# Gate and up matmuls of a two-layer trunk: the high and low part of x side by side under one weight tile

## The chip, the cores and the metric

The kernel runs on one core of a Trainium2 chip. What counts is the device time of one execution in microseconds (us), from the start of the program to its end. Of the core's engines, TensorE (PE) does matmuls into PSUM, VectorE (DVE) and ScalarE (ACT) work element by element, GpSimd (POOL) does a few slow side jobs and issues some loads, and SyncE (SP) issues the weight loads. They run side by side and wait for each other by semaphores only.

## What is computed

A trunk of two layers on 256 tokens of 1,024 channels, all in float32. Each layer has a feed-forward block, a token mixer (pooling in the first layer, windowed attention in the second) and a second feed-forward block, each with a residual and a layer norm. Four feed-forward blocks with an inner width of 2,816 hold most of the work:

```python
def swiglu(x, w_gate, w_up, w_down):
    h = jax.nn.silu(x @ w_gate) * (x @ w_up)
    return h @ w_down

for i in range(DEPTH):
    x = post_norm(x, 0.5 * swiglu(x, ffn_w_gate[i, 0], ffn_w_up[i, 0], ffn_w_down[i, 0]), ln_g[i, 0], ln_b[i, 0])
    ...   # mixer and its norm
    x = post_norm(x, 0.5 * swiglu(x, ffn_w_gate[i, 1], ffn_w_up[i, 1], ffn_w_down[i, 1]), ln_g[i, 2], ln_b[i, 2])
```

## The kernel before

**Three matmuls for one.** A float32 product is made from reduced-precision pieces (type fp32r): ScalarE rounds a tile to its high part, VectorE subtracts to get the low part, and TensorE adds up high x high, high x low and low x high. The helper `three` (lines 1056 to 1059) does this: line 1057 is w_hi with x_hi, line 1058 w_hi with x_lo, line 1059 w_lo with x_hi. The stationary operand of gate and up is a 128x128 weight tile, the moving one x transposed, 256 tokens wide.

**Units.** The inner width is cut into 22 units of 128 channels. For unit u of a block f, `gate_up(f, u)` makes the gate (m = 0) and the up half (m = 1), each over 8 tiles of 128 channels k: 2 x 8 x 3 = 48 matmuls of 256 columns, both halves into one PSUM bank, `WORK + u % 2`. `ffn_down(f, u)` multiplies h by the down weights into the accumulator banks 0 to 3: 12 matmuls of 512 columns. Units 0 and 1 use the unsplit weights (`gate_up_raw`), whose outputs go to the same banks as the others'.

**Order on the engines.** It is written out by hand. TensorE runs gate_up(u) and then ffn_down(u-1), with a loop over units 2 to 17 and the last four written out; there the down parts are halved by token tile, so that after gate_up(20) only half a down part and gate_up(21) stand before the down part of unit 20. Beside it ScalarE makes, per unit, SiLU of the gate (line 471), the two high halves of unit u+2's gate and up weights (459), the high part of h (475) and of the next down weights (467). VectorE makes the product with up (728), the two low halves (720), the low part of h (733) and of the down weights (724). Semaphores tie them: `g_used` counts finished gate and up parts, `silu_done`, `hf_done`, `h_hi_done` and `h_lo_done` the steps of h; ffn_down waits for `h_lo_done`, and a gate_up waits for `hf_done` of the unit two before it, whose PSUM bank it takes. SyncE loads the next pair of units' weights when `g_lo_done` or `d_lo_done` says that a buffer is free.

**GpSimd** scales the pool weights (line 335) when they have landed, which is near the end of the first block, and then gb (341, 345); their load is issued once `d_lo_done` has reached the low part of unit 19's down weights.

**Between blocks** x is normalised, transposed by TensorE (`transposes`, line 1123, into banks 6 and 7) and split into xT_hi and xT_lo.

## Time and profile before

| | us |
|---|---|
| three runs | 917.87, 919.07, 919.52 |
| median | 919.07 |
| span of the profiled execution, first to last instruction | 916.1 |
| TensorE busy in it | 875.6 (96%) |
| VectorE busy | 540.4 (59%) |
| ScalarE busy | 380.1 (41%) |
| GpSimd busy | 76.3 (8%) |

The profiled execution is told by its span; its own time is not listed beside the three runs, whose median lies 3.0 us above the span. The mean granted clock of TensorE over the span is 0.992 of full speed (2.4 GHz). Records of matmuls overlap, and their ends are modelled, so the pace of TensorE is read from one start to the next, and not from the duration shown.

### The profile page before, as it was taken

How to read it: one execution, taken by the hardware profiler on the slowest of the kernel's cores; microseconds unless marked ns; L12 is line 12 of the kernel's file. 1: busy time of each engine (PE TensorE's matmuls, PEld its weight loads, DVE VectorE, ACT ScalarE, POOL GpSimd, SP SyncE). 2: the span in 40 equal slices, each digit the busy share in tenths (PEclk: the TensorE clock that was granted, in tenths of full speed). 3: DMA queues.
4: the chain of work that ended last, by engine and by line, in shares of the span. 5: the costliest groups of instructions: out<-in, count | busy, mean ns of one | idle time of the engine just before them, and what ended most of it. 6: DMA issues, size and time to landing. Idle time of an engine off the chain costs nothing.

```text
span 916.1 us, 14933 instructions
## 1 busy us (share of the span) xinstructions
PE 875.6 (96%) x5954; PEld 805.0 (88%) x5954; DVE 540.4 (59%) x758; ACT 380.1 (41%) x622; POOL 76.3 (8%) x71
## 2 busy tenths in 40 slices
PE   6999999997999999999999999988999999999995
PEld 6999999986999999998999999976766899999994
DVE  1764455488674455447665545568687775445445
ACT  2444344322444344333434433435575434434430
POOL 0020000066100000001040000023000100000001
PEclk9999999999999999999999999999999999999998
DMA  9886546254485555660865565450127096555501
GB/s 293 304 289 219 183 160 207 97 176 141 170 301 184 197 172 181 211 202 2 275 239 184 173 217 175 161 218 15 42 101 254 20 311 234 183 189 177 184 1 46
DMA packets 116275, 162.30 MB, mean 177 GB/s; under 512 B 3968, under 2 KB 97760, under 8 KB 116240
## 3 DMA queue, kind: packets, MB, share of 16 engines
q1 hardware_dynamic: 112656, 152.06, 49.2%
q0 software_dynamic: 2496, 9.44, 2.8%
q8 instruction: 24, 0.39, 0.2%
q10 hardware_dynamic: 1088, 0.32, 0.1%
q14 instruction: 11, 0.09, 0.0%
HBM read 160.75 MB, written 1.05 MB: 177 GB/s over the span
## 4 chain that ended last, share of the span: by engine, by line
PE 82%; DVE 10%; ACT 3%; POOL 2%; issue 1%; DMA 1%; SPq 0%; POOLq 0%; DVEq 0%; ACTq 0%
PE ps L1057 25%; PE ps L1058 25%; PE ps L1059 25%; PE ps L1073 5%; DVE stats L759 2%; DVE xn L758 2%; DMA raw_g<-in_ffn_w_up 1%; POOL rstd L356 1%; DVE xn L774 1%; PE ps L1123 1%; PE ps L943 1%; ACT silu L403 1%; PE ps L934 1%; PE ps L937 1%; POOL rstd L358 1%
## 5 line engine op out<-in xcount | busy, mean ns | idle before, releaser
L1059 PE MATMUL ps<-xT_hi,g_lo 128*128 128x256 f32 x1280 | 362.2, 283 | 0.0
L1058 PE MATMUL ps<-xT_lo,g_hi 128*128 128x256 f32 x1280 | 362.2, 283 | 0.0
L1057 PE MATMUL ps<-xT_hi,g_hi 128*128 128x256 f32 x1280 | 361.8, 283 | 0.0
L1057 PEld LDWEIGHTS ps<-xT_hi,g_hi 128*128 128x128 f32 x1280 | 245.4, 192 | 3.2
L1058 PEld LDWEIGHTS ps<-xT_lo,g_hi 128*128 128x128 f32 x1280 | 245.4, 192 | 3.1
L1059 PEld LDWEIGHTS ps<-xT_hi,g_lo 128*128 128x128 f32 x1280 | 245.4, 192 | 0.0
L720 DVE TENSOR_TENSOR g_lo<-raw_g,g_hi 128x1024 fp32r<-128x1024 f32 x171 | 206.5, 1247 | 42.0 <-ACT g_hi L459 41.9
L471 ACT ACTIVATE silu<-ps 128x256 f32<-128x256 f32 x88 | 33.8, 384 | 393.0 <-PE ps L1059 386.1
L728 DVE TENSOR_TENSOR hf<-silu,ps 128x256 f32<-128x256 f32 x88 | 37.0, 421 | 263.0 <-ACT silu L471 263.0
L459 ACT ACTIVATE g_hi<-raw_g 128x1024 fp32r<-128x1024 f32 x172 | 172.0, 1052 | 4.9 <-PE ps L943 4.4
L1057 PE MATMUL ps<-d_hi,hT_hi 128*128 128x512 f32 x352 | 138.7, 394 | 2.0 <-DVE hT_lo L733 2.0
L1058 PE MATMUL ps<-d_lo,hT_hi 128*128 128x512 f32 x352 | 137.9, 392 | 0.0
L1059 PE MATMUL ps<-d_hi,hT_lo 128*128 128x512 f32 x352 | 137.0, 389 | 0.0
L724 DVE TENSOR_TENSOR d_lo<-raw_d,d_hi 128x1024 fp32r<-128x1024 f32 x98 | 122.8, 1254 | 2.6 <-ACT d_hi L467 2.6
L467 ACT ACTIVATE d_hi<-raw_d 128x1024 fp32r<-128x1024 f32 x98 | 102.7, 1049 | 3.1 <-PE ps L1059 3.0
L1059 PEld LDWEIGHTS ps<-d_hi,hT_lo 128*128 128x128 f32 x352 | 66.1, 188 | 14.5
L1057 PEld LDWEIGHTS ps<-d_hi,hT_hi 128*128 128x128 f32 x352 | 66.4, 189 | 14.0 <-DVE hT_lo L733 2.4
L1058 PEld LDWEIGHTS ps<-d_lo,hT_hi 128*128 128x128 f32 x352 | 66.4, 189 | 10.6
L1073 PE MATMUL ps<-xf,raw_g 128*128 128x128 f32 x512 | 61.7, 282 | 3.8 <-DMA raw_g<-in_ffn_w_up 3.2
L1073 PEld LDWEIGHTS ps<-xf,raw_g 128*128 128x128 f32 x512 | 60.1, 197 | 5.4 <-DMA raw_g<-in_ffn_w_up 3.4
L733 DVE TENSOR_TENSOR hT_lo<-hf,hT_hi 128x256 fp32r<-128x256 f32 x88 | 43.5, 494 | 5.3 <-ACT hT_hi L475 5.3
L475 ACT ACTIVATE hT_hi<-hf 128x256 fp32r<-128x256 f32 x88 | 35.9, 408 | 11.9 <-DVE hf L728 11.9
(137 smaller groups left out, 548.9 us busy)
## 6 DMA issues: line engine op xcount, KB each, us to landing
raw_d<-in_ffn_w_down SPq DMA_DIRECT2D x87, 512.0 KB, 4.0
raw_g<-in_ffn_w_gate SPq DMA_DIRECT2D x43, 1024.0 KB, 5.3
raw_g<-in_ffn_w_up SPq DMA_DIRECT2D x43, 1024.0 KB, 7.8
raw_g<-in_attn_w_qkv SPq DMA_DIRECT2D x6, 1024.0 KB, 6.6
raw_d<-in_attn_w_o SPq DMA_DIRECT2D x8, 512.0 KB, 3.7
gb<-in_ln_g POOLq DMA_DIRECT2D x6, 512.0 KB, 5.2
gb<-in_ln_b POOLq DMA_DIRECT2D x6, 512.0 KB, 6.3
xn<-in_x SPq DMA_DIRECT2D x2, 512.0 KB, 7.2
```

Source lines behind the costliest of these rows:

```text
L459: act.activation(g_half(g_hi, X, half), src(G, half), ACT.Copy).then_inc(g_hi_done, 1)
L467: act.activation(d_hi[:, E % D_SLOTS, :], raw_d[:, (E // 2) % 2, E % 2, :], ACT.Copy).then_inc(d_hi_done, 1)
L471: act.activation(silu[:, u % 2, :], ps[:, WORK + u % 2, 0:S], ACT.Silu).then_inc(silu_done, 1)
L475: act.activation(hT_hi[:, (D0[f] + u) % D_SLOTS, :], hf[:, u % 2, :], ACT.Copy).then_inc(h_hi_done, 1)
L720: dve.tensor_tensor(g_half(g_lo, X, half), src(G, half), g_half(g_hi, X, half).bitcast(f32), ALU.subtract).then_inc(g_lo_done, 1)
L724: dve.tensor_tensor(d_lo[:, E % D_SLOTS, :], raw_d[:, (E // 2) % 2, E % 2, :], d_hi[:, E % D_SLOTS, :].bitcast(f32), ALU.subtract).then_in ...
L728: dve.tensor_tensor(hf[:, u % 2, :], silu[:, u % 2, :], ps[:, WORK + u % 2, S:2 * S], ALU.mult).then_inc(hf_done, 1)
L733: dve.tensor_tensor(hT_lo[:, slot, :], hf[:, u % 2, :], hT_hi[:, slot, :].bitcast(f32), ALU.subtract).then_inc(h_lo_done, 1)
L1057: pe.matmul(out_, l_hi, r_hi, start=start, stop=False)
L1058: pe.matmul(out_, l_hi, r_lo, start=False, stop=False)
L1059: return pe.matmul(out_, l_lo, r_hi, start=False, stop=stop)
L1073: last = pe.matmul(ps[:, WORK + u % 2, m * S + t * P:m * S + (t + 1) * P], raw_unit(G, m)[:, k, :], xf[:, t, k, :], start=i == 0, stop=i = ...
```

## The change

The high and low part of x^T become one tile `xT` with the two side by side for each k, so that x_hi and x_lo of one k are 512 columns in a row. In a wide unit one matmul of 512 columns with w_hi takes the place of two of 256: it writes w_hi x_hi to the lower half of a bank and w_hi x_lo to the upper half. The matmul w_lo x_hi, 256 columns, is added to the upper half. Gate and up then need a bank each, so a unit takes two banks (`unit_bank`), and units u and u+1 take all four work banks. The two halves must be added: ScalarE copies the upper halves of both banks into `gu` (`low_of`), and VectorE adds the lower halves to it (`gate_up_sum`). SiLU and the product read `gu` in SBUF instead of PSUM. Between them, ScalarE and VectorE do one half of unit u+2's weights where they did both behind SiLU and product.

Units 0 and 1 (unsplit weights) and 21, the last, are `DIRECT`: they keep their form, with the two banks of `unit_bank`. Since all four work banks are taken, the transposes between blocks go into the accumulator banks instead; their waits on xf, and one such wait in attention, are gone.

```diff
+DIRECT = (0, 1, UNITS - 1)
+WIDE = UNITS - len(DIRECT)
...
-        xT_hi = sb("xT_hi", [P, KT, S], f32r)
-        xT_lo = sb("xT_lo", [P, KT, S], f32r)
+        xT = sb("xT", [P, KT, 2, S], f32r)
+        xT_hi, xT_lo = xT[:, :, 0, :], xT[:, :, 1, :]
...
-        silu = sb("silu", [P, 2, S])
+        gu = sb("gu", [P, 2, 2, S])
...
+        def unit_bank(u, m):
+
+            return ps[:, WORK + 2 * (u % 2) + m, :]
...
             def silu_of(f, u, it=0):
+                if u in DIRECT:
+                    act.wait_ge(g_used, G0[f] + u + 1)
+                    gate = unit_bank(u, 0)[:, 0:S]
+                else:
+                    act.wait_ge(gu_done, WIDE * f + u - RAW_UNITS + 1 + 4 * it)
+                    gate = gu[:, u % 2, 0, :]
+                act.activation(gu[:, u % 2, 0, :], gate, ACT.Silu).then_inc(silu_done, 1)
+
+            def low_of(f, u, it=0):
+
                 act.wait_ge(g_used, G0[f] + u + 1 + 4 * it)
-                act.activation(silu[:, u % 2, :], ps[:, WORK + u % 2, 0:S], ACT.Silu).then_inc(silu_done, 1)
+                both = ps[:, WORK + 2 * (u % 2):WORK + 2 * (u % 2) + 2, :]
+                act.activation(gu[:, u % 2, :, :], both[:, :, S:2 * S], ACT.Copy).then_inc(low_done, 1)
...
-                silu_of(f, u, it)
-                if 1 <= u < UNITS - 2:
-                    g_split(f, u + 2, it)
-                elif f == 2 and u == UNITS - 2:
-                    g_split(None, 0)
+                ahead = (f, u + 2, it) if 1 <= u < UNITS - 2 else (None, 0) if f == 2 and u == UNITS - 2 else None
+                if u not in DIRECT:
+                    low_of(f, u, it)
+                if ahead and u not in DIRECT:
+                    g_split(*ahead, halves=(0,))
+                    silu_of(f, u, it)
+                    g_split(*ahead, halves=(1,))
...
+            def gate_up_sum(f, u, it=0):
+
+                dve.wait_ge(low_done, WIDE * f + u - RAW_UNITS + 1 + 4 * it)
+                both = ps[:, WORK + 2 * (u % 2):WORK + 2 * (u % 2) + 2, :]
+                dve.tensor_tensor(gu[:, u % 2, :, :], both[:, :, 0:S], gu[:, u % 2, :, :], ALU.add).then_inc(gu_done, 1)
...
-                dve.tensor_tensor(hf[:, u % 2, :], silu[:, u % 2, :], ps[:, WORK + u % 2, S:2 * S], ALU.mult).then_inc(hf_done, 1)
+                up = unit_bank(u, 1)[:, 0:S] if u in DIRECT else gu[:, u % 2, 1, :]
+                dve.tensor_tensor(hf[:, u % 2, :], gu[:, u % 2, 0, :], up, ALU.mult).then_inc(hf_done, 1)
...
-                pe.wait_ge((xf_lo_done, xf_up_done)[t], 8 * e + 8)
...
-                        last = three(ps[:, WORK + u % 2, m * S:(m + 1) * S], w_hi, w_lo,
-                                     xT_hi[:, k, :], xT_lo[:, k, :], k == 0, k == KT - 1)
+                        bank = unit_bank(u, m)
+                        if u in DIRECT:
+                            last = three(bank[:, 0:S], w_hi, w_lo, xT_hi[:, k, :], xT_lo[:, k, :], k == 0, k == KT - 1)
+                            continue
+                        if k == 0:
+                            pe.matmul(bank, w_hi, xT[:, k, :, :], start=True, stop=False)
+                        last = pe.matmul(bank[:, S:2 * S], w_lo, xT_hi[:, k, :], start=False, stop=False)
+                        if k > 0:
+                            last = pe.matmul(bank, w_hi, xT[:, k, :, :], start=False, stop=k == KT - 1)
...
-                    after(pe, (xf_lo_done, xf_up_done)[q], 8 * e + 4 * t)
                     for k in range(4 * q, 4 * q + 4):
-                        last = pe.transpose(ps[:, WORK + 2 + q, (k % 4) * P:(k % 4 + 1) * P], xn[:, t, k * P:(k + 1) * P], ident)
+                        last = pe.transpose(ACC[t][q][:, (k % 4) * P:(k % 4 + 1) * P], xn[:, t, k * P:(k + 1) * P], ident)
```

**TensorE, the first matmuls of a unit's gate part in the loop.** Before, each k has three matmuls of 256 columns:

```order
L1082 ISA
L1057 MATMUL ps<-xT_hi,g_hi 128x256
L1058 MATMUL ps<-xT_lo,g_hi 128x256
L1059 MATMUL ps<-xT_hi,g_lo 128x256
L1057 MATMUL ps<-xT_hi,g_hi 128x256
```

The same place in the changed kernel; x2 stands for the w_lo matmuls of k = 0 and k = 1, one after the other:

```order
L1121 ISA
L1132 MATMUL ps<-xT,g_hi 128x512
L1133 MATMUL ps<-xT,g_lo 128x256 x2
L1135 MATMUL ps<-xT,g_hi 128x512
L1133 MATMUL ps<-xT,g_lo 128x256
```

Of three matmuls per k two are left, a wide one and a narrow one, and from k = 1 on the narrow one comes first.

**VectorE, a unit in the loop.** Before, hf is the product, g_lo the two low halves of unit u+2, hT_lo and d_lo the low parts of h and of the down weights:

```order
L728 TENSOR_TENSOR hf<-silu,ps 128x256
L717 ISA
L720 TENSOR_TENSOR g_lo<-raw_g,g_hi 128x1024
L717 REGISTER_ALU
L720 TENSOR_TENSOR g_lo<-raw_g,g_hi 128x1024
L733 TENSOR_TENSOR hT_lo<-hf,hT_hi 128x256
L723 REGISTER_ALU
L724 TENSOR_TENSOR d_lo<-raw_d,d_hi 128x1024
```

The same unit in the changed kernel:

```order
L756 TENSOR_TENSOR gu<-ps,gu 128x512
L743 ISA
L746 TENSOR_TENSOR g_lo<-raw_g,g_hi 128x1024
L759 REGISTER_ALU
L761 TENSOR_TENSOR hf<-gu 128x256
L743 REGISTER_ALU
L746 TENSOR_TENSOR g_lo<-raw_g,g_hi 128x1024
L766 TENSOR_TENSOR hT_lo<-hf,hT_hi 128x256
L749 REGISTER_ALU
L750 TENSOR_TENSOR d_lo<-raw_d,d_hi 128x1024
```

The sum stands first, one low half moves ahead of the product, and the product reads gu alone.

**VectorE, units 20 and 21, behind the loop of the first block.** Before:

```order
L728 TENSOR_TENSOR hf<-silu,ps 128x256
L733 TENSOR_TENSOR hT_lo<-hf,hT_hi 128x256
L724 TENSOR_TENSOR d_lo<-raw_d,d_hi 128x1024
L728 TENSOR_TENSOR hf<-silu,ps 128x256
L733 TENSOR_TENSOR hT_lo<-hf,hT_hi 128x256
L758 SCALAR_TENSOR_TENSOR xn<-ps,ax 128x512
```

In the changed kernel:

```order
L756 TENSOR_TENSOR gu<-ps,gu 128x512
L761 TENSOR_TENSOR hf<-gu 128x256
L766 TENSOR_TENSOR hT_lo<-hf,hT_hi 128x256
L750 TENSOR_TENSOR d_lo<-raw_d,d_hi 128x1024
L761 TENSOR_TENSOR hf<-gu,ps 128x256
L766 TENSOR_TENSOR hT_lo<-hf,hT_hi 128x256
```

Unit 20 has the sum in front and a product from gu alone; unit 21 still takes up from PSUM.

## Rows read from the trace of the kernel before

**Rows 1.** The page's chain that ended last: shares of the span by engine.

```profile
PE 82%; DVE 10%; ACT 3%; POOL 2%; issue 1%; DMA 1%; SPq 0%; POOLq 0%; DVEq 0%; ACTq 0%
```

**Rows 2.** Timeline, TensorE, second block: start us, duration us, instruction, output<-inputs, shape.

```profile
302.62 0.28 PE L1059 MATMUL ps<-xT_hi,g_lo 128*128 128x256 f32 x1
302.74 0.40 PE L1057 MATMUL ps<-d_hi,hT_hi 128*128 128x512 f32 x1
...
305.49 0.28 PE L1057 MATMUL ps<-xT_hi,g_hi 128*128 128x256 f32 x1
...
311.24 0.40 PE L1057 MATMUL ps<-d_hi,hT_hi 128*128 128x512 f32 x1
```

**Rows 3.** Timeline, ScalarE and VectorE, the same unit; in brackets idle time before, and releaser.

```profile
302.94 0.38 ACT L471 ACTIVATE silu<-ps 128x256 f32<-128x256 f32 x1 [4.97 <-PE ps L1059]
303.22 2.00 ACT L459 ACTIVATE g_hi<-raw_g 128x1024 fp32r<-128x1024 f32 x2
303.36 0.42 DVE L728 TENSOR_TENSOR hf<-silu,ps 128x256 f32<-128x256 f32 x1 [3.72 <-ACT silu L471]
...
304.31 2.36 DVE L720 TENSOR_TENSOR g_lo<-raw_g,g_hi 128x1024 fp32r<-128x1024 f32 x2 [0.53 <-ACT g_hi L459]
...
305.12 0.41 ACT L475 ACTIVATE hT_hi<-hf 128x256 fp32r<-128x256 f32 x1
...
306.58 0.42 DVE L733 TENSOR_TENSOR hT_lo<-hf,hT_hi 128x256 fp32r<-128x256 f32 x1
```

**Rows 4.** Timeline, TensorE, down parts ending the first block: first and last of two stretches.

```profile
198.40 0.40 PE L1058 MATMUL ps<-d_lo,hT_hi 128*128 128x512 f32 x1
...
200.04 0.39 PE L1059 MATMUL ps<-d_hi,hT_lo 128*128 128x512 f32 x1
...
201.86 0.39 PE L1058 MATMUL ps<-d_lo,hT_hi 128*128 128x512 f32 x1
...
203.90 0.39 PE L1058 MATMUL ps<-d_lo,hT_hi 128*128 128x512 f32 x1
```

**Rows 5.** Groups by line: count, busy us, mean ns of one, idle us before.

```profile
L1058 PEld LDWEIGHTS ps<-xT_lo,g_hi 128*128 128x128 f32 x1280 | 245.4, 192 | 3.1
L758 DVE SCALAR_TENSOR_TENSOR xn<-ps,ax 128x512 f32<-128x512 f32 x24 | 16.4, 682 | 7.3 <-PE ps L1059 7.3
L496 ACT ACTIVATE xf<-ps 128x512 f32<-128x512 f32 x2 | 1.2, 597 | 13.2 <-PE ps L1123 13.2
```

**Rows 6.** Timeline, VectorE and GpSimd, end of first block; last row from the third.

```profile
177.00 1.22 DVE L724 TENSOR_TENSOR d_lo<-raw_d,d_hi 128x1024 fp32r<-128x1024 f32 x1
...
183.77 5.92 POOL L335 TENSOR_TENSOR raw_d<-raw_d,aux 128x1024 f32<-128x1024 f32 x2 [125.66 <-DMA raw_d<-in_pool_w]
187.38 2.59 DVE L733 TENSOR_TENSOR hT_lo<-hf,hT_hi 128x256 fp32r<-128x256 f32 x1
189.78 5.46 POOL L341 TENSOR_SCALAR gb<-gb 128x2048 f32<-128x2048 f32 x1
189.90 4.69 DVE L724 TENSOR_TENSOR d_lo<-raw_d,d_hi 128x1024 fp32r<-128x1024 f32 x1
194.51 0.41 DVE L728 TENSOR_TENSOR hf<-silu,ps 128x256 f32<-128x256 f32 x1
195.32 2.40 POOL L345 TENSOR_TENSOR gb<-gb,aux 128x1024 f32<-128x1024 f32 x1
195.40 2.60 DVE L733 TENSOR_TENSOR hT_lo<-hf,hT_hi 128x256 fp32r<-128x256 f32 x1 [0.48 <-ACT hT_hi L475]
...
475.66 2.62 DVE L733 TENSOR_TENSOR hT_lo<-hf,hT_hi 128x256 fp32r<-128x256 f32 x1
```

**Rows 7.** Waits of TensorE (total us, times, longest), then its timeline, end of first block.

```profile
PE ps L1057 <- DVE hT_lo L733: 2.0, 2, 1.4
...
181.32 0.40 PE L1057 MATMUL ps<-d_hi,hT_hi 128*128 128x512 f32 x1
...
198.06 0.50 PE L1057 MATMUL ps<-d_hi,hT_hi 128*128 128x512 f32 x1 [0.63 <-DVE hT_lo L733]
```

More of the change, by code:

```diff
@@ L140, in trunk_kernel @@
         d_used = sem("d_used")
+        low_done = sem("gate_up_low_read")
+        gu_done = sem("gate_up_read")
         silu_done = sem("silu_done")
@@ L451, in _, with g_split @@
         def _(act):
-            def g_split(f, u, it=0):
+            def g_split(f, u, it=0, halves=(0, 1)):
                 X, G, src = split_unit(f, u)
-                act.wait_ge(g_in[(G // 2) % 2], 32 * (G // 4 + 1) + 32 * it)
-                after(act, g_used, (G0[f] + u - 3 if f is not None and u < 4 else G - 1) + 4 * it)
-                for half in range(2):
+                if halves[0] == 0:
+                    act.wait_ge(g_in[(G // 2) % 2], 32 * (G // 4 + 1) + 32 * it)
+                    after(act, g_used, (G0[f] + u - 3 if f is not None and u < 4 else G - 1) + 4 * it)
+                for half in halves:
                     act.activation(g_half(g_hi, X, half), src(G, half), ACT.Copy).then_inc(g_hi_done, 1)
@@ L477, in unit @@
             def unit(f, u, it=0):
-                silu_of(f, u, it)
-                if 1 <= u < UNITS - 2:
-                    g_split(f, u + 2, it)
-                elif f == 2 and u == UNITS - 2:
-                    g_split(None, 0)
+                ahead = (f, u + 2, it) if 1 <= u < UNITS - 2 else (None, 0) if f == 2 and u == UNITS - 2 else None
[5 more added lines that the diff above has]
+                    g_split(*ahead, halves=(1,))
+                else:
+                    silu_of(f, u, it)
+                    if ahead:
+                        g_split(*ahead)
                 h_hi_of(f, u, it)
@@ L493, in channel_major @@
                     act.wait_ge(tr_done, 4 * e + 2 * t + 2)
-                    bank = ps[:, WORK + 3, :].rearrange("p (k s) -> p k s", k=4)
+                    bank = ACC[t][1].rearrange("p (k s) -> p k s", k=4)
                     if e == 0:
@@ L735, in unit @@
             def unit(f, u, it=0):
-                h_of(f, u, it)
-                if 1 <= u < UNITS - 2:
-                    g_split(f, u + 2, it)
-                elif f == 2 and u == UNITS - 2:
-                    g_split(None, 0)
+                ahead = (f, u + 2, it) if 1 <= u < UNITS - 2 else (None, 0) if f == 2 and u == UNITS - 2 else None
+                if u not in DIRECT:
+                    gate_up_sum(f, u, it)
+                    if ahead:
+                        g_split(*ahead, halves=(0,))
+                    h_of(f, u, it)
+                    if ahead:
+                        g_split(*ahead, halves=(1,))
+                else:
+                    h_of(f, u, it)
+                    if ahead:
+                        g_split(*ahead)
                 h_lo_of(f, u, it)
@@ L794, in channel_major @@
                 dve.wait_ge(tr_done, 4 * e + 2 * t + 1)
-                bank = ps[:, WORK + 2, :].rearrange("p (k s) -> p k s", k=4)
+                bank = ACC[t][0].rearrange("p (k s) -> p k s", k=4)
                 if e == 0:
@@ L827, in _ @@
                         dve.wait_ge(lnT_ps, 1)
-                        dve.tensor_copy(lnT[:, :, :, :].rearrange("p a n k -> p (a n k)"), ps[:, 7, 0:96]).then_inc(lnT_done, 1)
+                        dve.tensor_copy(lnT[:, :, :, :].rearrange("p a n k -> p (a n k)"), ps[:, 7, S:S + 96]).then_inc(lnT_done, 1)
                     if f == 0 and u == 2:
@@ L1072, in gate_up_raw @@
                             pe.wait_ge((xf_lo_done, xf_up_done)[k // 4], 8 * e + 4 * t + k % 4 + 1)
-                        last = pe.matmul(ps[:, WORK + u % 2, m * S + t * P:m * S + (t + 1) * P], raw_unit(G, m)[:, k, :],
+                        last = pe.matmul(unit_bank(u, m)[:, t * P:(t + 1) * P], raw_unit(G, m)[:, k, :],
                                          xf[:, t, k, :], start=i == 0, stop=i == KT - 1)
@@ L1143, in _ @@
                     for a in range(2):
-                        last = pe.transpose(ps[:, 7, 48 * a:48 * (a + 1)], lnrow[:, a, :], ident[0:48, 0:48])
+                        last = pe.transpose(ps[:, 7, S + 48 * a:S + 48 * (a + 1)], lnrow[:, a, :], ident[0:48, 0:48])
                     last.then_inc(lnT_ps, 1)
```

2 lines of the change are left out of this document (1 added, 1 removed).

## The prediction

> **What bounds the kernel now.** I read the chain of waits first. TensorE holds 82% of the path to the end; VectorE has 10% and ScalarE 3%, nearly all of it in the short stretches between feed-forward blocks, where a layer norm stands between two runs of matmuls [rows 1]. So I then read TensorE's timeline in the middle of a block, unit by unit. What the reader is to see there is spacing, start to start, not duration: the records overlap (a 256-column matmul is shown 283 ns long but the next one starts 120 ns later).
>
> One unit is 48 matmuls of 256 columns (gate and up) and then 12 of 512 columns (down). The down part starts at 302.74 and the next gate part at 305.49: 2.75 us for 12, so 229.2 ns each. The gate part runs from 305.49 to 311.24: 5.75 us for 48, so 119.8 ns each [rows 2]. A unit is 8.50 us with no gap in it. VectorE and ScalarE finish their part of a unit long before TensorE wants it: after gate and up end at 302.74, the low part of h is ready at 307.00 (4.26 us), and TensorE asks for it 8.50 us after that end [rows 3]. Inside the blocks, therefore, the kernel is as long as TensorE's matmuls are at these spacings.
>
> **Part 1: two 256-column matmuls become one of 512.** A 256-column matmul costs 119.8 ns and two cost 239.6; one of 512 costs 229.2. Columns streamed are the same; what goes is one fixed cost per matmul. Each wide unit has 2 x 8 = 16 such pairs, there are 22 units in a block, units 0 and 1 (raw) and 21 (direct) stay as they are, so 19 wide units x 4 blocks = 76, and 76 x 16 = 1,216 pairs. The w_lo matmul (256 columns, upper half) stays at 119.8. Per pair 10.4 ns are saved: 1,216 x 10.4 ns = **12.6 us**. The unit becomes 16 x (229.2 + 119.8) = 5.58 us of gate and up, plus 2.75 of down: 8.33 us.
>
> The price of a 512-column matmul is the term on which everything hangs, since the saving is a small difference. Its bounds: in an undisturbed stretch ten starts from 201.86 to 203.90 are 9 steps in 2.04 us, 226.7 ns; in a stretch with VectorE and ScalarE at work eight starts from 198.40 to 200.04 are 7 steps in 1.64 us, 234.3 ns [rows 4]. That gives 12.9 or 5.3 ns a pair, **15.7 or 6.4 us**. I take 229.2, the mean over a whole down part of the same loop, where both kinds occur. The step from a short matmul to a long one, which the change makes 16 times a unit, is in the trace too: 302.62 to 302.74 is 120 ns, what any short one costs [rows 2].
>
> The rows put the fixed part at 13 to 16 ns: at the clock of this stretch (granted clock at its upper level, 2.4 GHz) 256 columns take 106.7 ns against 119.8, and 512 take 213.3 against 229.2. The Trainium skill (TensorE: Matmul & The Clock Gate, § Wait — 56ns, not 53.3ns?) puts it at about 2.5 ns a matmul. By that rule the change would save 1,216 x 2.5 ns, an estimate of 3.0 us. The rows disagree with that price in every unit, so I go by them.
>
> **Part 2: the added work beside TensorE.** A wide unit gets a ScalarE copy of the low halves (512 elements a row out of PSUM) and a VectorE add (512 elements, PSUM and SBUF). Neither is in the trace; the nearest rows are the ScalarE copy of 512 elements out of PSUM, 597 ns, and the VectorE operation on 512 elements of PSUM and SBUF, 682 ns on average [rows 5]. In sum 0.60 and 0.68 us per unit on engines that are idle 4 to 5 us of each unit. In latency, counted from the end of gate and up (T), with handovers of 0.04 to 0.08 us as in [rows 3]: copy T+0.20 to 0.80, add to 1.55, first g_hi half in between (0.72 to 1.77), SiLU to 2.05, first g_lo half 1.84 to 3.05, product to 3.37, second g_hi half to 3.0, second g_lo half 3.3 to 4.5, hT_hi to 3.8, hT_lo to 4.87. It was 4.26, so 0.6 us later, and TensorE wants it at T + 2.75 + 5.58 = 8.33. Cost nothing, with 3.5 us to spare. Near a block's end, where half a down part is held back, the demand comes at T + 1.38 + 5.58 = 6.96, still 2.1 us to spare. In units 2 and 3 VectorE also makes the residual and, in the first block, the rotary tables; at worst the low part of h then comes some 1.5 us before it is asked for. Bound from above: the copy and add twice as long put 1.3 us on this latency, still nothing. Loads are triggered by the g_lo and d_lo halves, which come 0.6 us later, with whole units of lead.
>
> **Part 3: the end of the first block.** Here the trace shows the only two waits of TensorE for h inside a block, 2.0 us in all: 1.4 for unit 19's, which is ready at 189.97, and 0.63 for unit 20's at 198.06 [rows 6, 7]. The cause is GpSimd. From 183.77 to 197.72 it scales the pool weights and gb, and VectorE operations with both inputs in SBUF then take much longer: hT_lo 2.59 and 2.60 us where it took 0.42, d_lo 4.69 where it took 1.22 [rows 6]. The product hf (one input in PSUM) at 194.51 keeps its 0.41 us beside it. The change turns the product of a wide unit into SBUF times SBUF, so it joins the slow kind. The Trainium skill says the same (SBUF — State Buffer, § Who interferes with whom: a VectorE instruction with two SBUF inputs contends with a GpSimd instruction that reads SBUF, one with at most one SBUF input does not), and the trace agrees: 0.41 us against 2.60.
>
> Step by step, with T the end of unit 19's gate and up, 181.32 before [rows 7]: GpSimd starts when the pool weights land, which hangs on d_lo ended at 178.22 (5.4 after its unit's end); that comes 0.6 us later in a unit that is 0.17 shorter, so GpSimd starts at T+3.2 instead of T+2.45. Unit 19: second g_lo half slow, to 6.7; hT_lo slow, to 9.3; TensorE wants it at 6.96: **2.4 us** instead of 1.4. Then d_lo slow to 13.9, unit 20's add 14.5, SiLU 14.9, its product slow (2.6, as hT_lo) to 17.5, hT_hi 17.95, hT_lo 18.4; TensorE, 2.4 us late, wants it at 16.5: **1.95 us** instead of 0.63. Together 4.3 instead of 2.0: **+2.3 us**. Bounds: GpSimd late enough that unit 19's low part escapes it gives about 0; each slow operation a full GpSimd operation longer gives +5. The same meeting occurs once in the third block (hT_lo of 2.62 us at 475.66 [rows 6]), where a whole down part still hides it; up to 1 us may be lost there, which I leave to the range.
>
> **Part 4: the rest.** Transposes move to the accumulator banks and lose their waits on xf; the raw matmuls behind them wait for the same xf, so nothing goes and nothing comes. Unit 21 and the raw units keep three matmuls and a product from PSUM.
>
> **Sum.** The profiled execution's span is 916.1 us, the median of the three runs 919.07, so 3.0 us lie around the span; the sum is made as a difference and put on the median. 919.07 - 12.6 + 2.3 = **908.8 us**.
>
> **The rivals.**
> - *A wide matmul is at the slow pace.* With the copy, the add and the splits beside it each costs 234.3 ns: saving 6.4 us; with 2.3 to 5 lost at the first block's end, 915.0 to 917.6, say 915.5. For it: the slow steps occur where the other engines work. Against: in the same loop the mean is 229.2.
> - *It is at the fast pace and the end of the block loses nothing.* 919.07 - 15.7 = 903.4. For it: the last steps of each down part go at that pace. Against: the product is certain to become an SBUF-only operation there.
> - *The fixed cost is not per matmul.* If the 13 to 16 ns hang on the change of columns or operand rather than on the instruction, a saving of 2.5 to 3 ns a pair is left (by the page above 3.0 us): 919.07 - 3.0 + 2.3 = 918.4, no measurable change.
> - *Slower: the mixture exposes a weight load.* A load is shown 192 ns long [rows 5], more than the 120 ns of a short matmul and less than the 229 of a long one. If, in a stream that alternates, the load for the long one could not hide behind the short one, up to 192 - 120 = 72 ns a pair would be added: 1,216 x 62 ns net = 75 us, with the 2.3 above 996 us. It decides against the change from 10.4 ns of exposure a pair on (8.5 with the 2.3 us above). Against it: loads already start 120 ns apart in the all-short stream, and the step from short to long at 302.62 shows nothing exposed. A late handover would have to pass T+8.46, 3.6 us above my estimate, to do the same.
>
> **How the numbers follow.** Forecast (900 to 913, centre 908.8) 0.62; slow pace 0.16; fast pace 0.11; fixed cost elsewhere 0.07; slower 0.04. What a measurement of this kernel can tell from no change is about 0.2%, 1.8 us: under 917.2 is faster, over 920.9 slower. Forecast, fast pace and nearly all of the slow pace are faster: 0.89; same 0.07; slower 0.04. The range leaves out the last two cases and the upper end of the slow pace: 903 to 916.
>
> **What would show it.** In the profile after: 1,216 matmuls of 512 columns on xT, the next start 229 ns behind; 256-column starts 120 ns behind; a unit of 8.33 us from SiLU to SiLU; hT_lo ending 4.9 us behind the end of gate and up; no wait of TensorE for hT_lo inside blocks but two at the end of the first, 4.3 us together, with a product of some 2.6 us beside GpSimd. Wrong if the long matmul's step is above 234 or below 226 ns, if units show gaps, or if the waits at the first block's end differ from 4.3 by more than 2 us.

## The result, and the profile after

| | before | after |
|---|---|---|
| median of the runs, us | 919.3 (917.9 to 920.2, 4 runs) | 908.8 (908.4 to 909.2, 4 runs) |
| profiled execution, span, us | 916.1 | 906.6 |
| its mean granted clock | 0.992 | 0.988 |

The ratio is 0.9881, interval 0.9867 to 0.9895: 1.2% faster, 10.5 us by the medians and 9.5 by the spans. The forecast was 908.8 with a range of 903 to 916. Where both are listed, an execution's time lies 1.8 us above its span (908.44 and 906.6 for the one of after). The profiled execution of before, with a span of 916.1, was therefore the fastest of its kernel, 917.9 us, and so was that of after; the prediction's 3.0 us around the span are these 1.8 and 1.2 by which the median lay above it.

The page of the changed kernel: busy time of the engines, the shares of the chain that ended last, and the groups that matter (line, engine, operation, count, busy us, mean ns of one, idle us before).

```profile
PE 864.1 (95%) x4738; PEld 739.8 (82%) x4738; DVE 591.1 (65%) x834; ACT 428.9 (47%) x698; POOL 76.4 (8%) x71
...
PE 80%; DVE 11%; ACT 3%; issue 2%; POOL 2%; DMA 1%; SPq 0%; POOLq 0%; DVEq 0%; ACTq 0%
...
L1135 PE MATMUL ps<-xT,g_hi 128*128 128x512 f32 x1064 | 379.3, 396 | 0.0
L1133 PE MATMUL ps<-xT,g_lo 128*128 128x256 f32 x1216 | 314.4, 279 | 0.0
...
L756 DVE TENSOR_TENSOR gu<-ps,gu 128x512 f32<-128x512 f32 x76 | 52.6, 692 | 209.6 <-ACT gu L491 209.6
...
L491 ACT ACTIVATE gu<-ps 128x512 f32<-128x512 f32 x76 | 45.4, 597 | 280.2 <-PE ps L1135 280.2
L1096 PE MATMUL ps<-d_hi,hT_hi 128*128 128x512 f32 x352 | 138.6, 394 | 4.3 <-DVE hT_lo L766 4.3
```

TensorE still bounds the kernel: 80% of the chain, where it was 82% [rows 1]. The new kinds are there: 1,064 wide matmuls here and 152 of k = 0 on another line (1,216 together), and 76 copies and 76 sums, whose idle time in front (280 and 210 us) says that they wait for TensorE and not TensorE for them.

One unit of the second block on TensorE, as in [rows 2] (start us, duration us, engine, line, operation, output<-inputs, shape):

```profile
293.99 0.39 PE L1096 MATMUL ps<-d_hi,hT_hi 128*128 128x512 f32 x1
...
296.71 0.39 PE L1132 MATMUL ps<-xT,g_hi 128*128 128x512 f32 x1
296.94 0.40 PE L1133 MATMUL ps<-xT,g_lo 128*128 128x256 f32 x2
297.17 0.40 PE L1135 MATMUL ps<-xT,g_hi 128*128 128x512 f32 x1
297.40 0.28 PE L1133 MATMUL ps<-xT,g_lo 128*128 128x256 f32 x1
297.52 0.40 PE L1135 MATMUL ps<-xT,g_hi 128*128 128x512 f32 x1
297.76 0.28 PE L1133 MATMUL ps<-xT,g_lo 128*128 128x256 f32 x1
297.88 0.40 PE L1135 MATMUL ps<-xT,g_hi 128*128 128x512 f32 x1
...
302.30 0.39 PE L1096 MATMUL ps<-d_hi,hT_hi 128*128 128x512 f32 x1
...
305.02 0.39 PE L1132 MATMUL ps<-xT,g_hi 128*128 128x512 f32 x1
```

Read the starts. The gate part runs from 296.71 to 302.30, 5.59 us where it took 5.75. Over the units of the block the step from wide to narrow is 233.5 ns on the mean (225 to 242) and that from narrow to wide 116.1 (111 to 121). The down part, 302.30 to 305.02, is 2.72 us where it was 2.75. The unit is 8.31 us (293.99 to 302.30) instead of 8.50.

The same unit on ScalarE and VectorE, as in [rows 3]; in brackets the idle time before, and what ended it:

```profile
294.19 0.60 ACT L491 ACTIVATE gu<-ps 128x512 f32<-128x512 f32 x1 [3.77 <-PE ps L1135]
...
294.81 0.69 DVE L756 TENSOR_TENSOR gu<-ps,gu 128x512 f32<-128x512 f32 x1 [3.14 <-ACT gu L491]
...
296.91 0.42 DVE L761 TENSOR_TENSOR hf<-gu 128x256 f32<-128x256 f32 x1
...
298.38 0.41 DVE L766 TENSOR_TENSOR hT_lo<-hf,hT_hi 128x256 fp32r<-128x256 f32 x1
```

Gate and up end at T = 293.99, hT_lo at 298.79, T + 4.80, and TensorE asks for it at T + 8.31.

The end of the first block, as in [rows 6]: VectorE, then GpSimd, then TensorE's waits for hT_lo (the row of the waits: total us, times, longest; under it the three places on the timeline).

```profile
183.91 3.43 DVE L746 TENSOR_TENSOR g_lo<-raw_g,g_hi 128x1024 fp32r<-128x1024 f32 x1
187.27 2.57 DVE L766 TENSOR_TENSOR hT_lo<-hf,hT_hi 128x256 fp32r<-128x256 f32 x1
189.76 4.68 DVE L750 TENSOR_TENSOR d_lo<-raw_d,d_hi 128x1024 fp32r<-128x1024 f32 x1
194.37 0.68 DVE L756 TENSOR_TENSOR gu<-ps,gu 128x512 f32<-128x512 f32 x1
195.53 2.34 DVE L761 TENSOR_TENSOR hf<-gu 128x256 f32<-128x256 f32 x1 [0.48 <-ACT gu L485]
198.35 0.42 DVE L766 TENSOR_TENSOR hT_lo<-hf,hT_hi 128x256 fp32r<-128x256 f32 x1 [0.48 <-ACT hT_hi L495]
```

```profile
183.76 5.79 POOL L343 TENSOR_TENSOR raw_d<-raw_d,aux 128x1024 f32<-128x1024 f32 x2 [123.70 <-DMA raw_d<-in_pool_w]
189.64 5.46 POOL L349 TENSOR_SCALAR gb<-gb 128x2048 f32<-128x2048 f32 x1
195.19 2.40 POOL L353 TENSOR_TENSOR gb<-gb,aux 128x1024 f32<-128x1024 f32 x1
```

```profile
PE ps L1096 <- DVE hT_lo L766: 4.3, 3, 2.1
...
189.90 0.51 PE L1096 MATMUL ps<-d_hi,hT_hi 128*128 128x512 f32 x1 [2.12 <-DVE hT_lo L766]
...
198.83 0.50 PE L1096 MATMUL ps<-d_hi,hT_hi 128*128 128x512 f32 x1 [1.51 <-DVE hT_lo L766]
...
476.63 0.49 PE L1096 MATMUL ps<-d_hi,hT_hi 128*128 128x512 f32 x1 [0.72 <-DVE hT_lo L766]
```

The operations with two SBUF inputs that start behind one of GpSimd's are slow, the product of unit 20 now among them (2.34 us at 195.53). The sum at 194.37, with PSUM as one input, keeps its 0.68 us. TensorE waits 4.3 us instead of 2.0 [rows 7], the third time in the third block.

**Where the 9.5 us of the spans are.** The second block has neither a wait for h nor a change of clock, so it gives the loop by itself. I take it from the second tile's transposes at its start to those at its end, before (first two rows) and after (last two):

```profile
233.38 1.07 PE L1123 MATMUL ps<-cst,xn 128*128 128x128 f32 x8 [0.40 <-issue]
...
419.59 1.11 PE L1123 MATMUL ps<-cst,xn 128*128 128x128 f32 x8 [0.72 <-DVE xn L774]
```

```profile
234.25 1.06 PE L1168 MATMUL ps<-cst,xn 128*128 128x128 f32 x8 [0.44 <-DVE xn L814]
...
416.88 1.11 PE L1168 MATMUL ps<-cst,xn 128*128 128x128 f32 x8 [0.72 <-DVE xn L814]
```

That is 186.21 and 182.63: 3.58 us less in a block, 14.3 in four.

The waits for hT_lo give back more than the 2.3 us that their rows show. A wait is shown from the modelled end of the matmul before it, and that lies behind the point where the next one would start; the second step after a wait is long as well (0.34 us at 189.90 instead of 0.23). What they cost is read from e5 and e3 below, the two kernels without these waits. From the first down matmul to the second tile's transposes the kernel before takes 205.17 us and e5 202.70, so its waits cost 2.5 us. After takes 203.36 there and e3 199.01, 4.4 us, and another 1.0 in the third block (191.11 and 190.08). The changed kernel loses 2.9 us more than the kernel before.

The rest is the clock, and it goes both ways. These are the stretches from 15 to 22 us, before and then after: stretch, us, busy us and count of PE, PEld, DVE, ACT and POOL, granted clock, DMA share, GB/s.

```profile
15.00:22.00 7.00, 5.83 (x52) 5.83 (x53) 2.35 (x4) 2.81 (x6) 0.00 (x0) 1.00 1.08 356
```

```profile
15.00:22.00 7.00, 6.05 (x28) 6.05 (x29) 0.69 (x1) 0.46 (x1) 0.00 (x0) 0.51 1.09 355
```

The profiled execution of before had the upper level of the clock there (2.4 GHz), that of after the lower one (1.2 GHz): 28 matmuls start in the stretch instead of 52, and the first down matmul starts at 30.89 instead of 28.21, 2.7 us later. But before has a stretch at the lower level too, in attention. Here it is, and below it the same place of e5, which has the same attention and the upper level:

```profile
700.90:704.30 3.40, 3.40 (x9) 2.35 (x8) 2.63 (x4) 0.05 (x1) 0.00 (x0) 0.50 0.44 139
```

```profile
700.10:703.50 3.40, 3.36 (x13) 1.79 (x12) 2.59 (x4) 0.01 (x1) 0.00 (x0) 1.00 0.46 144
```

The section around it, from 666.65 to 713.37, takes before 46.72 us, after 45.38 and e5 45.39, so the profiled execution of before lost 1.3 us. That of after lost 0.4 us between its third block and attention, at the lower level from 609.1 to 612.5 (607.99 to 618.14 is 10.15 us, in before and e3 the same section takes 9.79 and 9.80). Sum: -14.3 + 2.9 + 2.7 - 1.3 + 0.4 = -9.6, against -9.5 measured. The spans thus hold 1.8 us of clock, which differs between executions of one kernel as well (last section).

### The profile page after: what moved, and what is told of

It reads as the page before. It is cut to its first block, busy times and chain, and to the rows that moved or that the text cites. A ratio compares the mean times of both kernels' runs of the same rounds, so it can differ in the third digit from the quotient of the medians.

```text
span 906.6 us, 12819 instructions
## 1 busy us (share of the span) xinstructions
PE 864.1 (95%) x4738; PEld 739.8 (82%) x4738; DVE 591.1 (65%) x834; ACT 428.9 (47%) x698; POOL 76.4 (8%) x71
## 4 chain that ended last, share of the span: by engine, by line
PE 80%; DVE 11%; ACT 3%; issue 2%; POOL 2%; DMA 1%; SPq 0%; POOLq 0%; DVEq 0%; ACTq 0%
PE ps L1135 27%; PE ps L1133 15%; PE ps L1096 9%; PE ps L1098 9%; PE ps L1097 9%; PE ps L1112 4%; PE ps L1132 4%; DVE stats L799 2%; DVE xn L798 2%; DMA raw_g<-in_ffn_w_up 1%; POOL rstd L364 1%; DVE xn L814 1%; PE ps L1168 1%; PE ps L983 1%; ACT gu L411 1%
## 5 line engine op out<-in xcount | busy, mean ns | idle before, releaser
L1135 PE MATMUL ps<-xT,g_hi 128*128 128x512 f32 x1064 | 379.3, 396 | 0.0
L1133 PE MATMUL ps<-xT,g_lo 128*128 128x256 f32 x1216 | 314.4, 279 | 0.0
L1133 PEld LDWEIGHTS ps<-xT,g_lo 128*128 128x128 f32 x1216 | 229.3, 189 | 12.7
L1135 PEld LDWEIGHTS ps<-xT,g_hi 128*128 128x128 f32 x1064 | 200.1, 188 | 40.9
L746 DVE TENSOR_TENSOR g_lo<-raw_g,g_hi 128x1024 fp32r<-128x1024 f32 x171 | 213.2, 1251 | 23.0 <-ACT g_hi L468 22.8
L756 DVE TENSOR_TENSOR gu<-ps,gu 128x512 f32<-128x512 f32 x76 | 52.6, 692 | 209.6 <-ACT gu L491 209.6
L468 ACT ACTIVATE g_hi<-raw_g 128x1024 fp32r<-128x1024 f32 x172 | 179.3, 1050 | 6.1 <-PE ps L983 4.7
L491 ACT ACTIVATE gu<-ps 128x512 f32<-128x512 f32 x76 | 45.4, 597 | 280.2 <-PE ps L1135 280.2
L1132 PE MATMUL ps<-xT,g_hi 128*128 128x512 f32 x152 | 59.8, 393 | 0.0
L766 DVE TENSOR_TENSOR hT_lo<-hf,hT_hi 128x256 fp32r<-128x256 f32 x88 | 41.2, 469 | 5.3 <-ACT hT_hi L495 5.3
L364 POOL TENSOR_SCALAR rstd<-mv 128x1 f32<-128x1 f32 x12 | 10.9, 906 | 329.0 <-DVE mv L805 329.0
```

The source lines that it names most:

```text
L468: act.activation(g_half(g_hi, X, half), src(G, half), ACT.Copy).then_inc(g_hi_done, 1)
L746: dve.tensor_tensor(g_half(g_lo, X, half), src(G, half), g_half(g_hi, X, half).bitcast(f32), ALU.subtract).then_inc(g_lo_done, 1)
L756: dve.tensor_tensor(gu[:, u % 2, :, :], both[:, :, 0:S], gu[:, u % 2, :, :], ALU.add).then_inc(gu_done, 1)
L1132: pe.matmul(bank, w_hi, xT[:, k, :, :], start=True, stop=False)
L1133: last = pe.matmul(bank[:, S:2 * S], w_lo, xT_hi[:, k, :], start=False, stop=False)
L1135: last = pe.matmul(bank, w_hi, xT[:, k, :, :], start=False, stop=k == KT - 1)
```

## The experiments

The kernels of the first group (the first four) ran beside 13 runs of the kernel before with a median of 920.5 us, the others beside 13 with 919.6; beside after it was 919.3. A difference between medians of two groups has up to 1.2 us of play by that, and the second block, which repeats within 0.02 us, tells more. The theory is that a fixed cost per matmul is saved, that the added work lies under TensorE, and that GpSimd makes the waits at the end of block one. The rivals are that the gain is of another origin (banks, order, handovers), that the side work costs something, and that the waits come of the longer latency as such.

| kernel | median, us | ratio to before, interval | waits for hT_lo, us | second block, us |
|---|---|---|---|---|
| before | 920.5 / 919.6 | | 2.0 | 186.21 |
| after | 908.8 | 0.988, 0.987 to 0.990 | 4.3 | 182.63 |
| e1 wide matmul split again | 917.2 | 0.997, 0.996 to 0.998 | 2.0 | 185.05 |
| e4 long ones in a row | 905.3 | 0.985, 0.982 to 0.987 | 2.7 | 182.13 |
| e2 gb scaled early | 904.3 | 0.984, 0.981 to 0.986 | 0.7 | 182.65 |
| e3 GpSimd in slots | 901.9 | 0.981, 0.978 to 0.984 | 0 | 182.64 |
| e5 slots in the kernel before | 917.1 | 0.997, 0.996 to 0.998 | 0 | 186.19 |
| e6 e3, side work twice | 901.9 | 0.981, 0.979 to 0.983 | 0 | 182.65 |
| e8 e3, last unit wide | 905.6 | 0.985, 0.983 to 0.987 | 2.0 | 183.24 |
| e7 e3 and e4 together | 901.0 | 0.979, 0.977 to 0.982 | 0 | 182.13 |

**e1: the wide matmul undone, all else kept.** For k = 1 to 6 it is two of 256 columns again, 6 x 2 x 76 = 912 pairs.

```diff
-                        if k > 0:
-                            last = pe.matmul(bank, w_hi, xT[:, k, :, :], start=False, stop=k == KT - 1)
+                        if 0 < k < KT - 1:
+                            pe.matmul(bank[:, 0:S], w_hi, xT_hi[:, k, :], start=False, stop=False)
+                            pe.matmul(bank[:, S:2 * S], w_hi, xT_lo[:, k, :], start=False, stop=False)
+                        if k == KT - 1:
+                            last = pe.matmul(bank, w_hi, xT[:, k, :, :], start=False, stop=True)
```

> The changed kernel with its banks, copies and sums, but for k = 1 to 6 the wide matmul is two of 256 columns again, as in the kernel before: 12 of the 16 pairs of each wide unit, 912 pairs in all. Fixed cost per matmul: a wide and a narrow step were 233.5 + 116.2 = 349.7 ns in the changed kernel, three narrow ones 359.5, so 9.8 ns a pair, 8.9 us: 917.7 us, gate and up of a unit 5.71 us instead of 5.59. Rival, the gain came from elsewhere (banks, order of the splits, transposes): it stays near 908.8.

917.2 (915.1 to 918.6, 10 runs), 8.4 us more than after. The block is 2.42 us longer than after's, or 10.6 ns for each of its 228 pairs. Gate and up take 5.70 us, 9.2 ns more a pair; the rest lies for the most part in the down parts, 2.74 us where after has 2.72. The kernel keeps the copy, the sum, the four banks and the moved transposes, so the gain hangs on the number of matmuls and not on those. One wait for hT_lo of 2.0 us is left, unit 19's, instead of three of 4.3; that the others go because a unit is 0.13 us longer is likely but not shown.

**e4: sixteen wide matmuls in a row, then sixteen narrow.** The rows of after left open whether the order of long and short costs anything.

```diff
+                    for m in range(2):
+                        for k in range(KT):
+                            pe.matmul(unit_bank(u, m), g_half(g_hi, X, m)[:, k, :], xT[:, k, :, :], start=k == 0, stop=False)
+                    for m in range(2):
+                        for k in range(KT):
+                            last = pe.matmul(unit_bank(u, m)[:, S:2 * S], g_half(g_lo, X, m)[:, k, :], xT_hi[:, k, :], start=False, stop=k == KT - 1)
```

> The changed kernel, with the 16 wide matmuls of a unit in a row and then its 16 narrow ones. If a long step behind a long one costs 226.9 ns and a short behind a short 119.8, as in the down parts and in the kernel before, a pair costs 346.7 instead of 349.7 ns: minus 48 ns a unit, with some 24 ns back for the slower first long steps behind short ones: 907.0 us. If the price of a matmul does not depend on its neighbours: 908.8. Slower, 910 or more, if many short ones in a row delay the long ones behind them more than that.

905.3, 3.5 less than after, where 2 were expected. TensorE's timeline of a unit:

```profile
294.81 3.79 PE L1127 MATMUL ps<-xT,g_hi 128*128 128x512 f32 x16
298.43 2.08 PE L1130 MATMUL ps<-xT,g_lo 128*128 128x256 f32 x16
300.34 0.40 PE L1096 MATMUL ps<-d_hi,hT_hi 128*128 128x512 f32 x1
...
303.09 1.30 PE L1127 MATMUL ps<-xT,g_hi 128*128 128x512 f32 x5
```

Sixteen wide steps take 3.62 us, 226 ns each, and sixteen narrow ones 1.91, 119 ns each. Gate and up together are 5.54 us, so a pair is 346.2 ns, in after 349.3 (5.589 us for 16). But the down part that now follows short ones is slower, 300.34 to 303.09 = 2.75 us, so the unit is only 0.03 us and the block 0.50 us shorter than after's: 2.0 in four. The remaining 1.5 us are the waits, 2.7 where after has 4.3. That they would shrink was not expected. It is the meeting with GpSimd that e2 shows next: here VectorE's g_lo half and GpSimd's scaling start at the same 183.76, the half takes 1.22 us instead of 3.43, and unit 19's wait is gone. Left are 0.63 us for unit 20, 1.24 for unit 21 and 0.81 in the third block.

**e2: GpSimd scales gb early.** In the first block the scaling of gb, 5.46 + 2.40 us of GpSimd behind the pool weights, goes in front of them, to about 66 us, where TensorE then waits for nothing of it.

```diff
-
-                    for k in range(POOL_UNITS):
-                        raw = raw_d[:, (D_POOL // 2) % 2, k, :]
-                        if k == 0:
-                            gp.wait_ge(d_in[(D_POOL // 2) % 2], 32 * (D_POOL // 4 + 1))
-                        gp.tensor_tensor(raw, raw, aux[:, 0:D], ALU.mult).then_inc(d_scaled, 1)
...
+                if n == 0:
+                    for k in range(POOL_UNITS):
+                        raw = raw_d[:, (D_POOL // 2) % 2, k, :]
+                        if k == 0:
+                            gp.wait_ge(d_in[(D_POOL // 2) % 2], 32 * (D_POOL // 4 + 1))
+                        gp.tensor_tensor(raw, raw, aux[:, 0:D], ALU.mult).then_inc(d_scaled, 1)
```

> The changed kernel, with GpSimd's scaling of gb in the first block ahead of its scaling of the pool weights instead of behind, so that it runs early in the block. GpSimd theory: the wait of TensorE for unit 20's low part (1.51 us at 198.83) goes, that for unit 19's (2.12 us) stays, the one in the third block (0.72) stays: 908.8 - 1.5 = 907.3 us. Rival, the added sum and copy themselves make VectorE late at the block's end: both waits stay, 908.8.

904.3, 3 us below what was expected: both waits of the first block are gone, where only unit 20's should have been. VectorE, then GpSimd, of this kernel:

```profile
183.58 1.22 DVE L746 TENSOR_TENSOR g_lo<-raw_g,g_hi 128x1024 fp32r<-128x1024 f32 x1
184.72 2.63 DVE L766 TENSOR_TENSOR hT_lo<-hf,hT_hi 128x256 fp32r<-128x256 f32 x1
187.27 3.41 DVE L750 TENSOR_TENSOR d_lo<-raw_d,d_hi 128x1024 fp32r<-128x1024 f32 x1
```

```profile
183.67 5.93 POOL L354 TENSOR_TENSOR raw_d<-raw_d,aux 128x1024 f32<-128x1024 f32 x2 [108.14 <-DMA raw_d<-in_pool_w]
```

The g_lo half starts 0.09 us ahead of GpSimd's scaling and takes 1.22 us. In after it started at 183.91, 0.15 behind GpSimd's 183.76, and took 3.43. hT_lo therefore ends at 187.35 here and at 189.84 there. A quarter of a microsecond between two engines that don't know of each other decides over 2 us. The other kernels bear it out: in e4 the two start together and the half takes 1.22 us, in e1 it starts 0.20 behind and takes 3.44.

**e3: all of GpSimd's work in slots.** As e2, and in blocks one and three each scaling of gb waits for the low part of h of unit 5 or 6; the pool weights, one by one, wait for that of unit 19 or 20. GpSimd then works while VectorE has nothing that TensorE needs soon.

```diff
+                    gp.wait_ge(h_lo_done, UNITS * (2 if n else 0) + 6)
...
+                    gp.wait_ge(h_lo_done, UNITS * (2 if n else 0) + 7)
...
+                        gp.wait_ge(h_lo_done, UNITS - 2 + k)
```

> As the last, and GpSimd's slow operations start only behind a unit's low part of h: gb scaled behind units 5 and 6 (first and third block), the pool weights behind units 19 and 20. GpSimd theory: all three waits of TensorE for hT_lo go, 4.3 us together: 904.5 us, span about 902.3. Rival, lateness from the added work itself: 907 to 909.

901.9 (900.2 to 902.9), 2.6 below what was expected, and no wait for hT_lo is left in the whole trace. GpSimd and VectorE:

```profile
184.92 3.28 POOL L357 TENSOR_TENSOR raw_d<-raw_d,aux 128x1024 f32<-128x1024 f32 x1 [104.79 <-DVE hT_lo L769]
190.32 2.41 POOL L357 TENSOR_TENSOR raw_d<-raw_d,aux 128x1024 f32<-128x1024 f32 x1 [2.12 <-DVE hT_lo L769]
```

```profile
188.90 0.43 DVE L764 TENSOR_TENSOR hf<-gu 128x256 f32<-128x256 f32 x1 [0.48 <-ACT gu L488]
189.81 0.42 DVE L769 TENSOR_TENSOR hT_lo<-hf,hT_hi 128x256 fp32r<-128x256 f32 x1 [0.48 <-ACT hT_hi L498]
```

The product of unit 20 takes 0.43 us instead of 2.34. By the medians it is 6.9 us under after, by the spans 6.5 (906.6 and 900.1). These are the waits, which cost 5.4 by the stretches given above though their rows show 4.3, 0.7 at the start (the clock granted from 15 to 22 us is 0.76, and the first down matmul starts at 30.15) and 0.35 between the third block and attention, where after had the lower clock. Nothing is left over, so the waits are 5.4 us of it and the clock 1.1.

**e5: the same slots in the kernel before.** It tells whether the slots or the change earn that.

```diff
+                    gp.wait_ge(h_lo_done, UNITS * (2 if n else 0) + 6)
...
+                    gp.wait_ge(h_lo_done, UNITS * (2 if n else 0) + 7)
...
+                        gp.wait_ge(h_lo_done, UNITS - 2 + k)
```

> The kernel before, with GpSimd's slow operations gated as in e3_gated. GpSimd theory: TensorE's two waits for hT_lo at the end of the first block (1.4 and 0.63 us) go: 2.0 us less than the kernel before. Since the same edit took 4.3 us of waits from the changed kernel, 2.3 us of it are then the price of the change at these places. Rival: these waits belong to the block's end itself and stay.

917.1, 2.5 us less than the kernel before; its two waits, 2.0 us, are gone. So the change is worth 917.1 - 901.9 = 15.2 us with GpSimd out of the way, from medians of two groups, and 10.5 with it in the way. The stretches between the marks used above give 14.3 for the first (3.69, 3.55, 3.57 and 3.51 in the four blocks).

**e6: e3 with the side work twice.** A second ScalarE copy and a second VectorE sum of the same halves in each wide unit, into memory that nothing reads then.

```diff
+                act.activation(qT[:, 6:8, :], both[:, :, S:2 * S], ACT.Copy)
...
+                dve.tensor_tensor(vd[:, u % 2].rearrange("p g e d -> p (g e d)").rearrange("p (a s) -> p a s", a=2), both[:, :, 0:S], gu[:, u % 2, :, :], ALU.add)
```

> e3_gated with the added side work twice: a second ScalarE copy of the low halves and a second VectorE sum, into unused buffers, ahead of the real ones, 1.3 us more latency in each of 76 wide units. Theory, side work is hidden behind TensorE: hT_lo ends 6.2 instead of 4.9 us behind the end of gate and up, asked for at 8.3 (7.0 for unit 19): no change, 901.9 within 1 us. Rival, the side work is part of the path or slows TensorE by sharing SBUF or PSUM: 2 us or more; fully on the path 76 x 1.3 = 99 us.

901.9, the time of e3, and the block is 182.65 beside 182.64. VectorE's rows of a unit (gate and up ended at 296.82):

```profile
298.14 0.69 DVE L760 TENSOR_TENSOR vd<-ps,gu 128x512 f32<-128x512 f32 x1 [2.89 <-ACT gu L495]
298.75 0.68 DVE L761 TENSOR_TENSOR gu<-ps,gu 128x512 f32<-128x512 f32 x1
...
302.01 0.42 DVE L771 TENSOR_TENSOR hT_lo<-hf,hT_hi 128x256 fp32r<-128x256 f32 x1
```

hT_lo ends 5.61 us behind the end of gate and up instead of 4.80 (6.2 expected), still 2.7 before TensorE asks for it. The rival that ScalarE's and VectorE's extra work costs something inside a block falls. The step from wide to narrow is 233.6 ns here and 233.7 in e3, so that work doesn't set its pace either.

**e8: e3 with the last unit wide too.** There the cover is shortest: no gate part follows, only the held down matmuls.

```diff
-DIRECT = (0, 1, UNITS - 1)
+DIRECT = (0, 1)
```

> e3_gated with unit 21, the last of a block, wide too. TensorE has only one down part (2.75 us) between its gate and up and its own down part. Theory, the handover is hidden only where there is cover: matmuls save 0.16 us a block, hT_lo comes some 3.4 us behind the end of gate and up (no weight halves between), 0.6 us too late, so 4 x (0.6 - 0.16) = 1.8 us: 903.7 us, and a wait of TensorE for hT_lo in each block. Rival, the handover has slack there too: 901.3.

905.6, where 903.7 was expected. The waits of TensorE and one of the four places:

```profile
PE ps L1099 <- DVE hT_lo L769: 2.0, 4, 0.5
...
407.50 0.50 PE L1099 MATMUL ps<-d_hi,hT_hi 128*128 128x512 f32 x1 [0.51 <-DVE hT_lo L769]
```

The wait is shown as 0.51 us and costs 0.78: from the matmul before it (406.61) to this one are 0.89 us where 0.23 are usual, and the next comes 0.34 later (407.84). Less the 0.17 of the unit's saved pairs (16 x 10 ns) that is 0.61, and block two is 0.60 us longer than in e3. The four blocks together give 2.3 us of the 3.4 by which the spans differ (903.5 and 900.1); 1.1 come from the start (first down matmul at 31.21 instead of 30.15). The last entry of `DIRECT` earns its place.

**e7: e3 and e4 together.**

> e3_gated and e4_grouped together. Theory: the two gains are independent; a unit is 8.28 instead of 8.32 us (measured in e4_grouped), 76 x 0.036 = 2.7 us: 901.9 - 2.7 = 899.2 us, no wait for hT_lo. Rival, the gain of e4_grouped came from shorter waits alone (2.7 instead of 4.3 us): then 901.9.

901.0 (899.8 to 904.0), where 899.2 was expected. Between it and e3 the medians don't decide, 0.9 us with runs 4 us apart. The second block does: 182.13 against 182.64, 0.5 us less and 2.0 in four, the same as e4 over after. The expectation of 2.7 us took the unit's gain as 0.036 us, a difference of two rounded readings; the block gives 0.50 / 19 = 0.026. Its profiled execution, at 904.0 the longest of its four, was granted 0.52 from 15 to 22 us, e3's 0.76, and had the lower level once more from 691.1 to 694.5. By the median it is the fastest kernel here, 2.1% under the kernel before.

## Why the prediction was right, and where it was only nearly so

**Part 1, two of 256 become one of 512: right as a sum, by two prices that were off against each other.** Gate and up take 5.59 us (5.58 forecast), and a pair of wide and narrow steps 349.3 ns (349.0); 10.2 ns a pair are saved, where 10.4 were forecast. The price of 229.2 was a mean of a down part, and what a wide step costs turns out to depend on its neighbours: 233.5 ns with a narrow one behind it, half a nanosecond short of the bound of 234 at which the prediction called itself wrong, and 226 in a row (e4). The narrow step then takes 116.1 instead of 119.8. Over 1,216 pairs the first error is +5.2 us and the second -4.5, so they cancel but for less than 1 us, which was not foreseen. That the fixed cost hangs on the instruction is shown by e1: 9.2 ns a pair come back in gate and up with the split, and 10.6 with the down parts. By the rule of the Trainium skill of about 2.5 ns a matmul (TensorE: Matmul & The Clock Gate, § Wait — 56ns, not 53.3ns?) e1 would have moved the time by 2.3 us, an estimate of 912 x 2.5 ns. It moved it by 8.4 by the medians and 9.7 by the blocks (2.42 x 4), so the measurement decides against that figure for this stream, in which every matmul comes with a weight load of its own.

**Not in the sum: the down steps.** The block lost 3.58 us. Part 1 gives 304 pairs x 10.2 ns = 3.11; most of the rest, 0.4 us, 1.6 in four blocks, is down parts of 2.724 instead of 2.747 us. Step by step through the down parts of the second block (medians): before, the first five steps, behind 48 short ones, take 233, 236, 228, 233 and 230 ns and the others 226 or 227; in after, behind an alternation, only the first is longer (231). In e4, behind 16 short ones, it is the first five again (233, 236, 229, 233, 231). So the order in front of the part makes the difference; why it does is not shown. It also corrects a reading in the prediction: the slow stretch from 198.40 on [rows 4], put down to VectorE and ScalarE at work, lies right behind short matmuls and a wait, and the fast one far behind them.

**Part 2, the added work is hidden: right.** hT_lo came at T + 4.80 (4.87 forecast), and doubling the work (e6) changed neither block nor median. e8 shows where the cover ends: in the last unit the same work costs 0.6 us a block more than its pairs save.

**Part 3, the end of the first block: right in mechanism, and in size by three terms instead of two.** Forecast were waits of 2.4 and 1.95 us and up to 1 us in the third block left to the range; shown are 2.12, 1.51 and 0.72. Their sum, 4.3, is that of the forecast because the third block, which the sum put at nothing, makes up for the smaller two. What the waits cost is more than their rows show, 5.4 us, against 2.5 before: 2.9 more, where 2.3 were forecast. The steps came as forecast: with T = 180.66 the slow hT_lo of unit 19 ends at T + 9.18 (9.3), the slow product of unit 20 at T + 17.21 (17.5), its hT_lo at T + 18.1 (18.4). The product took 2.34 us and not 2.6, since what such an operation takes is not a price of its own: it ends 0.3 us behind the end of the GpSimd operation that it meets, here 197.87 behind 197.59. That GpSimd is the cause is shown by e2, e3 and e5, which move only its work. What the step didn't see is how finely it hangs: with a GpSimd start a quarter of a microsecond later against VectorE, unit 19's wait would be gone (e2, and e4 by chance). The bound of about 0 that the prediction had named for a late GpSimd was nearer than it looked.

**Part 4, the rest: right.** The section between the third block and attention and attention itself differ between the kernels by less than 0.4 us once the clock is taken off; the 0.1 us that the sum of the spans leaves is within that.

**The rivals.** The slow pace falls as a rival for the time (the pair is 349.3, not 354), though its wide step of 234.3 is nearly the one measured: the narrow step gives it back, and e4 (226 beside the same side work) and e6 show that ScalarE and VectorE aren't its cause. The fast pace holds for wide steps in a row only, and its time of 903.4 needs GpSimd away as well, which is near e2 and e3. The fixed cost elsewhere falls with e1. An exposed weight load would have added up to 72 ns to a pair; narrow to wide takes 111 to 121 ns, so nothing is exposed.

**How much of the hit is luck.** A good part. Inside Part 1 +5.2 and -4.5 us nearly cancel. The sum left out the down steps (-1.6), 0.6 us of the waits' cost, and the clock, which in the two profiles is +3.1 on one side and -1.3 on the other and which no sum could have told. The medians carry less of it: the kernel before was granted 0.987 to 0.993 in its other runs. A forecast within 0.1 us of the median is more than the method gives, when the runs of one kernel lie 1 to 5 us apart and the median of the kernel before moved from 919.1 to 920.5 between groups. What the method gave is the terms: 12.5 us for 12.6 forecast in Part 1, 2.9 for 2.3 in Part 3.

## What to carry to other kernels

Where TensorE sets the time, read the cost of a matmul from start to start in the trace, with its columns taken off at the granted clock: here 9 to 20 ns stay on every instruction, and fewer, wider matmuls save them although no column goes. Read a wait's cost from start to start as well; its row shows some 0.3 us too little. When an edit turns a PSUM operand of VectorE into an SBUF one, look for each place where GpSimd works at the same time, and let the operation there end only when GpSimd's does. GpSimd's off-path work is best given a slot by a wait on the step that it must not meet: three such waits and an earlier place took away 4.3 us of shown waits on the changed kernel (5.4 from start to start) and 2.0 on the old one (2.5).
